# Second scan of a hybrid decoder step: odd chunks' preparation products on the other two 64x64 quarters of TensorE, and X summed on TensorE

## The reference

```python
def step(S, inp):
    r_t, w_t, k_t, v_t, kk_t, kka_t = inp
    sa = jnp.einsum("bhvk,bhk->bhv", S, kk_t)
    S = S * w_t[:, :, None, :] - sa[..., None] * kka_t[:, :, None, :] + v_t[..., None] * k_t[:, :, None, :]
    return S, jnp.einsum("bhvk,bhk->bhv", S, r_t)
```

## Time and profile before

| what | value |
|---|---|
| median of 3 runs | 4418.15 us (4413.96 to 4419.51) |
| profiled execution, its own time | 4375.91 us |
| its span | 4374.1 us |
| granted TensorE clock, mean | 0.911 |
| busy in the span: PE, PEld, DVE, ACT, POOL | 87%, 58%, 69%, 22%, 41% |
| second scan | about 1523 to 2105 us of the span |

### The profile page before, as it was taken

The page is one execution under the profiler, slowest core; times in us unless marked ns, Lnnn a source line. Parts: engine busy times, 40 slices in busy tenths (PEclk is TensorE's granted clock), DMA queues, the critical chain, the costliest instruction groups (busy, mean ns, idle before and its releaser), DMA issues. The chain is left out here.

```text
span 4374.1 us, 71420 instructions
## 1 busy us (share of the span) xinstructions
PE 3791.0 (87%) x28135; PEld 2533.3 (58%) x28135; DVE 3035.9 (69%) x5964; ACT 958.0 (22%) x2001; POOL 1802.3 (41%) x1489
## 2 busy tenths in 40 slices
PE   7976878799999888888778886668999999999998
PEld 6766765655555488787565464564544544455444
DVE  0454431678588658777777488876989788977777
ACT  1331230110133322222451013780000000000001
POOL 0007000057223034433225207735666566666665
PEclk9997879899999998898789997669999999999999
DMA  7542254389577467766549633459999999999998
GB/s 176 164 157 92 83 187 171 112 338 410 210 261 255 175 232 240 259 221 211 207 137 382 242 144 49 97 147 404 406 411 390 403 403 409 379 410 413 413 412 325
DMA packets 390906, 1152.47 MB, mean 263 GB/s; under 512 B 78174, under 2 KB 148387, under 8 KB 372995
## 3 DMA queue, kind: packets, MB, share of 16 engines
q0 software_dynamic: 207216, 687.87, 43.2%
q1 hardware_dynamic: 150628, 419.97, 25.9%
q10 hardware_dynamic: 32727, 40.05, 2.6%
HBM read 1044.67 MB, written 113.65 MB: 265 GB/s over the span
## 5 line engine op out<-in xcount | busy, mean ns | idle before, releaser
L2793 PE MATMUL x_vps<-l_c_v,x_w 128*128 128x512 f32 x1536 | 676.6, 602 | 38.4 <-DVE x_w L2842 38.4
L2785 PE MATMUL x_sps<-c_big,l_c_wo 128*128 128x384 f32 x2048 | 671.8, 490 | 26.8 <-DMA l_c_wo<-u_cols 23.6
L387 POOL DMA_INDIRECT l_w_ring<-u_rows,k_eidx x256 | 297.5, 1162 | 908.4 <-DVE l_w_dots L443 366.8
L387 POOL DMA_INDIRECT w_ring<-u_rows,k_eidx x384 | 478.2, 1245 | 402.2 <-DVE w_dots L443 238.5
L2785 PEld LDWEIGHTS x_sps<-c_big,l_c_wo 128*128 128x128 f32 x2048 | 391.5, 192 | 307.6 <-DMA l_c_wo<-u_cols 31.7
L460 DVE SCALAR_TENSOR_TENSOR l_c_share<-w_ring,w_wts,l_c_share 128x1024 f32<-128x1024 f32 x384 | 493.6, 1285 | 93.8 <-DMA w_ring<-v_rows,k_eidx 81.6
L2793 PEld LDWEIGHTS x_vps<-l_c_v,x_w 128*128 128x128 f32 x1536 | 296.4, 193 | 412.7 <-issue 361.4
L387 POOL DMA_INDIRECT w_ring<-v_rows,k_eidx x384 | 411.6, 1072 | 159.3 <-issue 109.6
L387 POOL DMA_INDIRECT l_w_ring<-v_rows,k_eidx x256 | 289.8, 1132 | 328.8 <-DVE l_w_yacc L460 264.8
L460 DVE SCALAR_TENSOR_TENSOR l_w_yacc<-l_w_ring,l_w_wts,l_w_yacc 128x1024 f32<-128x1024 f32 x256 | 328.9, 1285 | 28.0 <-DMA l_w_ring<-v_rows,k_eidx 19.4
L443 DVE CUSTOM_DVE_ANT_0 w_ring<-w_ring,w_h 128x1024 f32<-128x1024 f32 x256 | 302.9, 1224 | 38.4 <-DMA w_ring<-u_rows,k_eidx 26.2
(11 more groups left out here) (652 smaller groups left out, 6282.3 us busy)
## 6 DMA issues: line engine op xcount, KB each, us to landing
l_c_wo<-u_cols SPq DMA_DIRECT2D x64, 1024.0 KB, 9.4
l_c_v<-v_rows SPq DMA_DIRECT2D x32, 2048.0 KB
e_c_w<-w_tiles SPq DMA_DIRECT2D x54, 512.0 KB, 3.6
l_c_w<-w_tiles SPq DMA_DIRECT2D x54, 512.0 KB, 6.8
l_c_wo<-s_G SPq DMA_DIRECT2D x16, 1536.0 KB, 9.2
s_rw<-l_q_out SPq DMA_DIRECT2D x48, 384.0 KB, 5.2
s_G<-l_c_share ACTq DMA_DIRECT2D x8, 2048.0 KB, 7.9
s_zT<-l_pz ACTq DMA_DIRECT2D x30, 384.0 KB, 7.1
```

The source lines that it names most:

```text
L387: pool.indirect_dma_start(out=self.ring[:, r, :], out_offset=None, in_=self.A[table], in_offset=bass.IndirectOffsetOnAxis(ap=idx[:, s:s + ...
L2785: mm = pe.matmul(sps[n % 2][:, 0:ND * P], u[n % 4][:, k, :], hT[:, k, :], start=(k == 0), stop=(k == KT - 1))
L2793: mm = pe.matmul(vps[k][:, x * 512:(x + 1) * 512], w[:, e, k * P:(k + 1) * P], v[:, e, x * 512:(x + 1) * 512], start=(c == 0 and e == 0), ...
```

## The change

It works in the second scan alone (`crossed = NY == 2`; in the first, NY is 1 and everything stays).

1. In every preparation product the odd chunks change sides. `side_of(name, c)` says for each product in which half its inputs lie (`was`) and to which half its output goes (`now`), 1 meaning crossed. Where the two differ, the matmul runs from rows of one half to output partitions of the other, so on the two quarters that were unused. This holds for every product but an (1, 1) and P1, PT1 (0, 0), which stay on the diagonal. vn, bn, kn, rbT, rkT, GT and H come out uncrossed, so the chain is as before, but for where a chunk lies (`spot`).
2. In PSUM and SBUF even chunks come first, then odd ones: even in the first bank of a buffer, odd in the second (`in_ps`, `spot`). Evacuations write both blocks with one instruction (`by_bank`, `from_ps`).
3. X_l = product + X_(l-1) is now summed in PSUM: after the four products of a pair of chunks come four matmuls of the identity with X (`kept_too`). X1 to X5 move from VectorE (L1428) to ScalarE, as plain copies.
4. The six leaves are loaded so that odd chunks arrive crossed: three DMAs each (even chunks 128 x 6 x 64, and odd chunks for each half 64 x 6 x 64) in place of one of 128 x 768. rho is loaded as before and its odd chunks once more, crossed, into `rho_odd`.

```diff
+    crossed = NY == 2
...
+    come_out = {**{x: (1, 0) for x in ("ab", "abT", "akT", "vn", "bn", "kn", "rbT", "rkT", "GT", "H")}, "an": (1, 1), "Z": (0, 1), "P1": (0, 0), "PT1": (0, 0),
+                **{f"{x}{l}": (l % 2, (l - 1) % 2) for x in ("P", "PT") for l in range(2, LEVELS + 1)},
+                **{f"X{l}": ((l - 1) % 2, l % 2) for l in range(1, LEVELS + 1)}}
+    side_of = lambda name, c: come_out[name] if crossed and c % 2 else (0, 0)
...
-        prep += [(fill[l], "D" if fill[l] == "rbT" else "A"), (f"X{l}", "D")]
+        prep += [(fill[l], "D" if fill[l] == "rbT" else "A"), (f"X{l}", "A" if crossed else "D")]
...
+        spot = lambda c: col(c % 2 * (NC // 2) + c // 2) if crossed else col(c)
+        in_ps = lambda c: col(c % 2 * (512 // CL) + c // 2) if crossed else col(c)
...
+                src, dst = src.rearrange("p (k two l) -> two p k l", two=2, l=CL), by_bank(rw[p % 2][:, i, :])
+                sp.dma_start(dst[:, 0], src[0]).then_inc(landed, 16)
+                for h in range(2):
+                    sp.dma_start(dst[half(h), 1], src[1][half(1 - h)]).then_inc(landed, 16)
...
+                kept_too = crossed and name[0] == "X"
+                step = 2 if crossed else 1
+                for c0 in range(0, NC, step):
+                    tiles = []
+                    for c in range(c0, c0 + step):
+                        was, now = side_of(name, c)
+                        tiles += [(c, half(h ^ was), half(h ^ now)) for h in range(2)]
+                    for c, src, dst in tiles:
+                        turned_by = rhs is rho_of_pair and crossed and c % 2
+                        with_ = (ident[src, src] if rhs is None else rho_odd[j][src, col(c // 2)] if turned_by else
+                                 rhs[src, col(c)] if rhs is rho_of_pair else rhs[src, spot(c)])
+                        mm = pe.matmul(ps[slot_of[name]][dst, in_ps(c)], lhsT[src, spot(c)], with_, start=True, stop=not kept_too)
+                    for c, src, dst in tiles if kept_too else []:
+                        mm = pe.matmul(ps[slot_of[name]][dst, in_ps(c)], ident[src, src], X[src, spot(c)], start=False, stop=True)
                 mm.then_inc(pe_prep, 1)
```

More of the change, by code:

```diff
@@ L1105, in scan_pairs @@
     AT = Steps(*[f"std{g}" for g in range(NY)])
-    DP = Steps("ab", "abT", "X0", "akT", "X1", "X2", "X3", "X4", "rbT", "X5", "rkT")
+    DP = Steps(*[x for name, e in prep if e == "D" for x in ((name, "X0") if name == "abT" else (name,))])
     DC = Steps(*[f"{x}{c}" for c in range(NC) for x in "us"])
@@ L1135, in scan_pairs @@
         fin = sb("r_fin", [P, HD])
+        rho_odd = two("r_rho_odd", [P, n // 2]) if crossed else None
         ps = [psum(f"r_ps{j}", 512 * NY) for j in range(2)]
@@ L1171, in _, with load_leaf @@
         def _(sp):
+            def load_leaf(p, i, landed):
+                src = A["rw"][p, i, :, tokens]
+                if not crossed:
+                    sp.dma_start(rw[p % 2][:, i, :], src).then_inc(landed, 16)
+                    return
+                src, dst = src.rearrange("p (k two l) -> two p k l", two=2, l=CL), by_bank(rw[p % 2][:, i, :])
+                sp.dma_start(dst[:, 0], src[0]).then_inc(landed, 16)
+                for h in range(2):
+                    sp.dma_start(dst[half(h), 1], src[1][half(1 - h)]).then_inc(landed, 16)
             def load_early(p):
                 for i in FIRST_IN:
-                    sp.dma_start(rw[p % 2][:, i, :], A["rw"][p, i, :, tokens]).then_inc(ab_in[p % 2], 16)
+                    load_leaf(p, i, ab_in[p % 2])
                 for i in THEN_IN:
-                    sp.dma_start(rw[p % 2][:, i, :], A["rw"][p, i, :, tokens]).then_inc(rw_in[p % 2], 16)
+                    load_leaf(p, i, rw_in[p % 2])
             def load_late(p):
                 sp.dma_start(rw[p % 2][:, R_RHO, :], A["rw"][p, R_RHO, :, tokens]).then_inc(rho_in[p % 2], 16)
+                for h in range(2 if crossed else 0):
+                    src = A["rw"][p, R_RHO, half(1 - h), tokens].rearrange("p (k two l) -> two p k l", two=2, l=CL)
+                    sp.dma_start(rho_odd[p % 2][half(h), :].rearrange("p (k l) -> p k l", l=CL), src[1]).then_inc(rho_in[p % 2], 16)
                 sp.dma_start(dend[p % 2][:, :], A["dend"][p, :, pt.t0 // CL:pt.t0 // CL + NC]).then_inc(rho_in[p % 2], 16)
@@ L1264, in y_chunk @@
                     pe.matmul(out, state(c, p, half(h)), rw[j][half(h), R_RHO, col(c)], start=True, stop=False)
-                    pe.matmul(out, U[half(h), col(c)], rbT[j][half(h), col(c)], start=False, stop=False)
-                    mm = pe.matmul(out, vn[j][half(h), col(c)], rkT[j][half(h), col(c)], start=False, stop=True)
+                    pe.matmul(out, U[half(h), col(c)], rbT[j][half(h), spot(c)], start=False, stop=False)
+                    mm = pe.matmul(out, vn[j][half(h), spot(c)], rkT[j][half(h), spot(c)], start=False, stop=True)
                 return mm
@@ L1297, in turn @@
                     for h in range(2):
-                        mm = pe.matmul(ups[half(h), bank(c)], GT[j][half(h), col(c)], state(c, p, half(h)), start=True, stop=True)
+                        mm = pe.matmul(ups[half(h), bank(c)], GT[j][half(h), spot(c)], state(c, p, half(h)), start=True, stop=True)
                     mm.then_inc(pe_chain, 1)
@@ L1309, in turn @@
                     for h in range(2):
-                        pe.matmul(sps[half(h), bank(c)], kn[j][half(h), col(c)], vn[j][half(h), col(c)], start=True, stop=False)
+                        pe.matmul(sps[half(h), bank(c)], kn[j][half(h), spot(c)], vn[j][half(h), spot(c)], start=True, stop=False)
                     side.pe(pe, p, c)
@@ L1313, in turn @@
                     for h in range(2):
-                        mm = pe.matmul(sps[half(h), bank(c)], bn[j][half(h), col(c)], U[half(h), col(c)], start=False, stop=True)
+                        mm = pe.matmul(sps[half(h), bank(c)], bn[j][half(h), spot(c)], U[half(h), col(c)], start=False, stop=True)
                     mm.then_inc(pe_chain, 1)
@@ L1414, in _ @@
             V = nc.vector
-            mask = lambda i: masks[:, i, :].unsqueeze(1).broadcast_to([P, NC, CL])
+            mask = lambda i: masks[:, i, :].unsqueeze(1).unsqueeze(1).broadcast_to([P, 2 if crossed else 1, NC // 2 if crossed else NC, CL])
             def done(sem_, S, name, p, ins):
@@ L1425, in prep_batch @@
                 dve.wait_ge(pe_prep, PP.after(name, p))
[L1426 removed]
                 if name[0] == "X":
[L1428 removed]
+                    done(dve_prep, DP, name, p, V.tensor_tensor(X[:, :], ps[slot_of[name]][:, 0:n], X[:, :], ALU.add))
                     return
                 dst, m = {"ab": (Pn[0], 0), "abT": (Pt[0], 1), "akT": (akT, 2), "rbT": (rbT[j], 3), "rkT": (rkT[j], 4)}[name]
[L1431 removed]
+                done(dve_prep, DP, name, p, V.tensor_tensor(by_bank(dst[:, :]), from_ps(slot_of[name]), mask(m), ALU.mult))
                 if name == "abT":
```

21 lines of the change are left out of this document (13 added, 8 removed).

## The result

The changed kernel takes 4447.05 us (median of 4 runs, 4438.19 to 4458.09) against 4417.28 us before on the same chip: ratio 1.0073, interval 1.0052 to 1.0095. It is slower, by some 30 us, where 75 us of gain were forecast.

The account below looks back on a forecast made before the run. TensorE was taken to set the pace of chunks 1 to 8, VectorE that of 9 to 11. Turns -82, pair 0 -5, start +5, loads +7 sum to -75 us: 4343 us, own range 4315 to 4368, 8 in 10 4310 to 4426.

Parts of the forecast that it names:

- TensorE's sum for chunks 1 to 8: Chunks with preparation, second scan: chain and hand-overs 1.25 us, batches at 15 ns a record, tails; 36.6 us against 47.5.
- the 82 us: Total saving forecast for turns 0 to 6, at 11.7 us a turn, before costs of start and loads.
- The break-even: Preparation on TensorE: above 24.1 ns a record, the crossing costs TensorE more than it saves.
- The issue rival: Preparation batches: an issue limit just past 24.1 ns a record leaves almost no gain, 4417 us; chance 17%.
- The half-gain rival: Preparation batches: four quarters run at about 20 ns a record, from uneven queues or instruction fetch, 4370 us; chance 20%.
- The 4.8 us a turn: VectorE in each turn: five additions of X, 0.957 us each, leave it.
- ScalarE: Five copies of X, 4.1 us a turn, mostly hide; 1 us a turn left for places where they bind.
- Start: First product of the second scan: nine load issues on SP take 6 us, so the start slips by 5 us.
- Pair 0's preparation: Preparation before the first turn, 1530 to 1581 us: 5 us saved, between 0 and 12.
- SP's issues: Later leaf and rho loads: 18 issues, some 12 us, covered because loads are asked for over a turn ahead.
- DMA: 256-byte packets add 7 us a turn per engine; the ring covers part, costing 1 us a turn, 7 in all.
- The rival on the slower side: X batches: quarters sharing rows do not overlap for 64x64, so each doubles at 28.7 ns a record; 4461 us, chance 10%.

Follow-up runs that it names:

- crossing, X on VectorE, narrow: Changed kernel with chunks 6 to 11 crossed instead of the odd ones, X added on VectorE, second scan's gathered rows cut to 1 KB; ratio 0.9951 against the kernel before.
- no identity: The halves kernel without the identity products of X, ScalarE's copies kept; ratios 0.9947 and 0.9969 against the kernel before.
- halves: Changed kernel with chunks 6 to 11 crossed instead of the odd ones, loaded in 1536-byte pieces; ratios 1.0098, 1.0112 and 1.0105 against the kernel before.
- split loads: Kernel before with each leaf of the second scan fetched in three DMAs of 256-byte pieces, nothing crossed; ratio 1.0029.
- the last pair: Changed kernel (256-byte pieces) and halves (1536-byte pieces) run again on one chip; ratios 1.0108 and 1.0105 against the kernel before.
- late P + I, crossed: The halves kernel with X = (P + I) X, VectorE writing P + I just before X, no identity products; ratios 0.9963 and 1.0000 against the kernel before.
- whole loads: Changed kernel with each leaf fetched by one DMA in 3 KB pieces, so its data is not crossed; ratio 1.0116 against the kernel before.

## Why the prediction was wrong

**The step that failed is TensorE's sum for chunks 1 to 8**, with batches at 15 x 48 = 0.7 us (X 1.4): 36.6 us was forecast, 57.1 came (48.5 before). "I take 15 ns" was met at 2.4 GHz: 15.7. But 0.7 us a batch was made the price of 48 records, and it is only their run; that their instructions must arrive had no term. Chunks 0 to 8 of a turn carry some 1500 records before (1248 of preparation, nine chains of 24, tails), 11.7 blocks, at 4.6 us each 54 us; they took 8.9 + 47.5 = 56.4. TensorE at 28.7 ns was busy there and seldom stalled, but by this sum its supply was all but used up as well. With 240 records more, 13.6 blocks, the same sum gives 63 us, and the changed turn spends 7.9 + 57.1 = 65. The missing term is records per turn times 36 ns, and it does not shrink with the batches. The rows for it were there: 28135 records on 223 instruction packets, and TensorE's idle time on "issue", 2.8 us at the longest.

**The supply is not the whole miss.** The sum also took 15 ns for every batch, where 20.9 is the mean of the changed kernel's, and left the clock where it was. And with few stalls left (crossing, X on VectorE, narrow) chunks 1 to 8 still took 49.4 us. So the 82 us would not have come with instructions in time either; how the rest divides stays open.

**The break-even was drawn on the wrong axis.** 24.1 ns asked how fast the array takes records. The issue rival supposed a limit near that rate within a batch; there a record takes 15.7 ns. The rule of the Trainium skill, TensorEngine Tiling (Array Packing), section Instruction Overhead, would have given 25 ns by the prediction's estimate; the rows at 2.4 GHz show 15.7, so the measurement stands against reading it as a limit on issue, while its advice would have led to the right side of the decision. The half-gain rival named instruction fetch, but as 20 ns; as a mean it is above 30.

**VectorE: less work, no less time.** The 4.8 us a turn went (busy 224/350 x 77.2 = 49.3 us a turn against 53.9), but VectorE was not what the turn waited for: its s step now waits for TensorE.

**ScalarE**, 1 us: no run showed more; no identity keeps the copies and beats the kernel before.

**Chunks 9 to 11** stayed as they were, as forecast (12.1 us against 12.0). **Start:** from the load of the masks to the first product 7.05 us became 8.83 (1518.52 to 1527.35): 1.8 later, not 5; the nine issues took 5.7 us, as taken. **Pair 0's preparation** did not gain 5 us but lost: from first product to turn 0, 64.7 us in this execution against 50.3. It is nothing but TensorE's batches, and its idle time on "issue" there is 20.4 us against 5.3, which covers the difference.

**SP's issues** of the leaves, estimated at 12 us a turn, took 23 to 30 in turns 0 to 4, with single pairs of them up to 9.0 us; in halves, with pieces of 1536 bytes, they took 11 to 13. The cover of more than a turn held, and TensorE waited for no load in any turn. **DMA**, 1 us a turn: split loads say 0.3%, 13 us in all, where start and loads together were put at 12; the last pair says less. A term of the right size.

**The rival on the slower side** had place and sign, the doubled X batches, and the wrong mechanism: they do overlap at 15.7 ns, and cost because they are records. It was given 10%.

Open stays why a refill comes 3.5 us after the last one at least and mostly over 4.5, when a packet is on its way for 1.0 us and TensorE runs some 1.4 us after it has landed. That gathers lengthen it is shown, across chips; what the rest is made of is not. The granted clock of the crossed kernels is lower (0.78 to 0.87 against 0.89 to 0.92 in 1661 to 1990 us), and no run separates what that costs.

## What to carry to other kernels

Price small matmuls twice: by what the array takes for a record and by what their instructions need to arrive, here some 36 ns a record (matmul and weight load) beside heavy DMA traffic; the larger counts. If TensorE shows idle time on "issue" that comes back every 128 records, count its instructions: here fewer of them or less DMA traffic helped, and more of them cost though the array was not full. Removing the stalls need not bring the gain: the next bound may lie close behind. An identity product that saves VectorE an addition is dear for 64x64 tiles, here 7.8 us a pair against the 4.8 us of VectorE that it saved; P + I on VectorE does the same sum without identity records, for VectorE time like that of the additions.

## What the runs showed of the hardware that I had not expected

- TensorE's program comes in packets of 16.4 KB, 256 instructions, 128 records; ahead of them it stops after a multiple of 128 records, for up to 4.7 us (late P + I, crossed), with at least 3.47 us from block to block. Such a stall ends some 1.4 us after a packet of the instruction queue has landed (1.2 to 1.6 us in whole loads).
- With gathers of a quarter of the bytes (DMA share 0.36 instead of 0.73 in 1661 to 1990 us) the instruction packets start 4.03 us apart at the median instead of 4.65.
- Four quarters of the array take 64x64 records at 15.7 ns at 2.4 GHz and at 26.6 ns at 1.2 GHz, crossed ones among them; two quarters take them at 28.7 and 53 ns.
- An issue of 384 or 768 pieces of 256 bytes takes SP 0.4 to 0.7 us at the start of the second scan, and up to 7.3 us for a single one later, in the loads of pair 1.
